# The low parts of the stream and of the wide factors, moved to other byte distances from the weights

## The reference

```python
for l in range(DEPTH):                        # first block, kernel layers 0 and 1
    h = rms_norm(x, mix_pre_norm[l])
    m = hybrid_mixer(h, w_in[l], ...)         # delta rule, pooling, retention, three gated branches, w_out
    x = x + rms_norm(m, mix_post_norm[l])
    h = rms_norm(x, ffn_pre_norm[l])
    x = x + rms_norm(swiglu(h, ffn_gate[l], ffn_up[l], ffn_down[l]), ffn_post_norm[l])
...
for l in range(DEPTH):                        # second block, kernel layers 2 and 3
    u = rmsnorm(h, attn_norm[l])
    h = h + hybrid_mixer_2(u, positions, w_in[l], ...)   # three attentions, three gated branches, w_o
    u = rmsnorm(h, mlp_norm[l])
    h = h + jnp.square(jax.nn.relu(u @ w_up[l])) @ w_down[l]
return rmsnorm(h, final_norm)
```

## Time and profile before

| | |
|---|---|
| time, median of 3 runs | 1875.27 us (1874.95 to 1875.65) |
| profiled execution: span from first to last instruction | 1875.1 us |
| TensorE matmuls, busy | 1841.3 us, 15,964 instructions |
| TensorE weight loads, busy | 1750.7 us |
| VectorE busy | 1259.6 us |
| ScalarE busy | 956.6 us |
| GpSimd busy | 307.3 us |
| read from HBM | 305.00 MB, 163 GB/s over the span |

### The profile page before, as it was taken

The page is one execution under the profiler, slowest core; times in us unless marked ns, Lnnn a source line. Parts: engine busy times, 40 slices in busy tenths (PEclk is TensorE's granted clock), DMA queues, the critical chain, the costliest instruction groups (busy, mean ns, idle before and its releaser), DMA issues.

```text
span 1875.1 us, 37406 instructions
## 1 busy us (share of the span) xinstructions
PE 1841.3 (98%) x15964; PEld 1750.7 (93%) x15964; DVE 1259.6 (67%) x1676; ACT 956.6 (51%) x1381; POOL 307.3 (16%) x176
## 2 busy tenths in 40 slices
PE   7999999999999999999999999999999999999998
PEld 7989998998888999999989999999999899999998
DVE  6884677665689557777648865676547785577643
ACT  5634466444563445554545455565434445555533
POOL 0050221000003212200002542310002352230000
PEclk9999999999999999999999999999999999999999
DMA  6443354656445334555656553456555663446652
GB/s 238 157 159 113 125 169 158 214 184 196 154 145 172 113 123 149 178 194 181 204 189 196 193 170 126 147 182 198 185 189 181 206 195 126 136 158 203 189 187 96
DMA packets 92165, 317.66 MB, mean 169 GB/s; under 512 B 11744, under 2 KB 12896, under 8 KB 91744
## 3 DMA queue, kind: packets, MB, share of 16 engines
q1 hardware_dynamic: 91424, 314.69, 51.7%
q10 hardware_dynamic: 576, 0.57, 0.1%
HBM read 305.00 MB, written 1.05 MB: 163 GB/s over the span
## 4 chain that ended last, share of the span: by engine, by line
PE 83%; DVE 12%; ACT 3%; issue 1%; DMA 1%; SPq 0%; DVEq 0%; ACTq 0%
PE bank L2007 82%; DVE wlo L1131 4%; DVE area L1131 3%; DVE area L1137 2%; ACT area L634 1%; ACT whi L640 1%; PE bank L2571 1%; DMA raw<-in_weights 1%; DVE hl L1137 1%; DVE xT L1137 1%; DVE area L1651 0%; DVE area L1649 0%; PE bank L2592 0%; ACT L622 0%; PE bank L2226 0%
## 5 line engine op out<-in xcount | busy, mean ns | idle before, releaser
L1131 DVE TENSOR_TENSOR wlo<-raw,whi 128x1024 fp32r<-128x1024 f32 x518 | 668.6, 1305 | 412.6 <-ACT whi L640 412.3
L2007 PE MATMUL bank<-hh,whi 128*128 128x256 f32 x2928 | 830.0, 284 | 18.5 <-DVE wlo L1131 15.9
L2007 PE MATMUL bank<-hh,wlo 128*128 128x256 f32 x2928 | 814.4, 279 | 0.0
L2007 PE MATMUL bank<-hl,whi 128*128 128x256 f32 x2928 | 807.2, 279 | 0.0
L640 ACT CAST whi<-raw 128x1024 fp32r<-128x1024 f32 x572 | 589.3, 1046 | 398.8 <-PE bank L2007 351.9
L2007 PEld LDWEIGHTS bank<-hh,whi 128*128 128x128 f32 x2928 | 551.3, 188 | 33.8 <-DVE wlo L1131 18.7
L2007 PEld LDWEIGHTS bank<-hl,whi 128*128 128x128 f32 x2928 | 551.1, 190 | 1.4 <-issue 1.4
L2007 PEld LDWEIGHTS bank<-hh,wlo 128*128 128x128 f32 x2928 | 551.4, 188 | 0.0
L1787 POOL TENSOR_TENSOR area<-area 128x512 f32<-128x512 f32 (+4 forms) x86 | 135.1, 1578 | 567.3 <-DVE area L1137 250.6
L1787 POOL TENSOR_TENSOR wlo<-raw,whi 128x1024 fp32r<-128x1024 f32 x54 | 133.9, 2481 | 384.7 <-ACT whi L640 384.7
L2007 PE MATMUL bank<-FH,whi 128*128 128x256 f32 x640 | 180.1, 281 | 0.0
(11 more groups left out here) (132 smaller groups left out, 1907.4 us busy)
## 6 DMA issues: line engine op xcount, KB each, us to landing
raw<-in_weights SPq DMA_DIRECT2D x572, 512.0 KB, 4.0
area<-area SPq DMA_DIRECT2D x96, 64.0 KB, 3.6
area<-area SPq DMA_DIRECT2D x16, 128.0 KB, 3.9
cst<-in_const SPq DMA_DIRECT2D x1, 1188.0 KB, 7.9
cst<-in_const SPq DMA_DIRECT2D x1, 1024.5 KB, 5.6
xT<-in_x SPq DMA_DIRECT2D x4, 256.0 KB, 7.9
out<-xT SPq DMA_DIRECT2D x4, 256.0 KB, 2.9
area<-in_lev SPq DMA_DIRECT2D x2, 384.0 KB, 6.8
```

Of the source, the lines that this page charges most:

```text
L1131: return v.tensor_tensor(dst, x, y, op)
L2007: return e.matmul(ps, x, y, start=start, stop=stop, skip_group_check=skip)
```

## The change

Each layer gets its own `hh`, `hl`, `FH` and `FL`, at addresses set modulo 512 relative to the first weight byte. For the high parts the distance is 192 in every layer, as before. For the low parts it is taken from a list by layer:

| layer | `hh`, `FH` | `hl` | `FL` |
|---|---|---|---|
| before, all | 192 | 192 | 192 |
| 0 | 192 | 224 | 64 |
| 1 | 192 | 160 | 0 |
| 2 | 192 | 0 | 224 |
| 3 | 192 | 64 | 160 |

The tensors of the four layers lie over one another, as one tensor did before. The stream's place is 512 bytes longer, which moves all behind it (`RSB`, `SW`, the work area) by 512 bytes. `FL` begins 32 to 480 bytes later in the area than its slot. Nothing else is changed; instructions, order and waits are the same.

```diff
+HIGH_PHASE = 192
+STREAM_PHASE = (224, 160, 0, 64)
+FACTOR_PHASE = (64, 0, 224, 160)
...
+        whi_at = at[0]
         whi = sb("whi", [P, RING, 1024], F32R)
...
-        hh = sb("hh", [P, 8, T], F32R)
-        hl = sb("hl", [P, 8, T], F32R)
+        stream = at[0]
+        at[0] += 2 * 4 * 8 * T + 512
...
-        def slot_r(name, i, k):
-            return sb(name, [P, k, T], F32R, offset=region + 4096 * i)
+        def slot_r(name, i, k, behind=0):
+            return sb(name, [P, k, T], F32R, offset=region + 4096 * i + behind)
+
+        def from_weights(first, by):
+            return (whi_at + by - first) % 512
+
+        hh, hl = ([sb(f"{name}{L}", [P, 8, T], F32R, offset=stream + by + from_weights(stream, STREAM_PHASE[L] if by else HIGH_PHASE))
+                   for L in range(2 * DEPTH)] for name, by in (("hh", 0), ("hl", 8192)))
...
-        FH, FL = slot_r("FH", 0, 32), slot_r("FL", 8, 32)
+        FH, FL = ([slot_r(f"{name}{L}", i, 32, from_weights(region, FACTOR_PHASE[L] if i else HIGH_PHASE)) for L in range(2 * DEPTH)]
+                  for name, i in (("FH", 0), ("FL", 8)))
```

Every use of the four names takes the tensor of its layer, for example:

```diff
-                    h = act(hh[:, k, :], xT[:, k, :], AF.Copy, scale=GAIN[norm][:, k:k + 1])
+                    h = act(hh[int(norm[-1])][:, k, :], xT[:, k, :], AF.Copy, scale=GAIN[norm][:, k:k + 1])
...
-                    return mm3(bank[m // 2][:, m % 2 * T:m % 2 * T + T], job.first + k, 128 * m, FH[:, k, :], FL[:, k, :],
+                    return mm3(bank[m // 2][:, m % 2 * T:m % 2 * T + T], job.first + k, 128 * m, FH[L][:, k, :], FL[L][:, k, :],
```

More of the change, by code:

```diff
@@ L851, in merge @@
                 a.wait_ge(*gated(name, L, 2 * j))
-                act(FH[:, 2 * j:2 * j + 2, :], v3(pair(YY, j)), AF.Copy, scale=0.5).then_inc(*a_br.up("sum", L, j))
+                act(FH[L][:, 2 * j:2 * j + 2, :], v3(pair(YY, j)), AF.Copy, scale=0.5).then_inc(*a_br.up("sum", L, j))
             def by_rows(name, L, settle={}):
@@ L932, in product @@
                     a.wait_ge(*v_ffn.at("product", L, i))
-                    a.copy(FH[:, i, :], FT[:, 512 * (i % 4):512 * (i % 4) + T]).then_inc(*a_ffn.up("high", L, i))
+                    a.copy(FH[L][:, i, :], FT[:, 512 * (i % 4):512 * (i % 4) + T]).then_inc(*a_ffn.up("high", L, i))
                 def ffn(m0):
@@ L1081, in mlp_high @@
                     a.wait_ge(*a_ffn.at("square", L, m0))
-                    a.copy(FH[:, m0:m0 + 2, :], v3(f)).then_inc(*a_ffn.up("high", L, m0))
+                    a.copy(FH[L][:, m0:m0 + 2, :], v3(f)).then_inc(*a_ffn.up("high", L, m0))
                 def mlp(m0):
@@ L1184, in low @@
                 for k in (2 * j, 2 * j + 1):
-                    x = stt(hl[:, k, :], xT[:, k, :], GAIN[norm][:, k:k + 1], hh[:, k, :].bitcast(F32), OP.mult, OP.subtract)
+                    x = stt(hl[int(norm[-1])][:, k, :], xT[:, k, :], GAIN[norm][:, k:k + 1], hh[int(norm[-1])][:, k, :].bitcast(F32), OP.mult, OP.subtract)
                 x.then_inc(*v_norm.up("low", norm, j))
@@ L1414, in merge @@
                 v.wait_ge(*a_br.at("sum", L, j))
-                stt(FL[:, 2 * j:2 * j + 2, :], v3(pair(YY, j)), 0.5, FH[:, 2 * j:2 * j + 2, :].bitcast(F32), OP.mult, OP.subtract).then_inc(*v_br.up("merged", L, j))
+                stt(FL[L][:, 2 * j:2 * j + 2, :], v3(pair(YY, j)), 0.5, FH[L][:, 2 * j:2 * j + 2, :].bitcast(F32), OP.mult, OP.subtract).then_inc(*v_br.up("merged", L, j))
             def by_rows(name, L, settle={}):
@@ L1531, in ffn_low @@
                     v.wait_ge(*a_ffn.at("high", L, i))
-                    tt(FL[:, i, :], f_(i)[:, 0:T], FH[:, i, :].bitcast(F32), OP.subtract).then_inc(*v_ffn.up("low", L, i))
+                    tt(FL[L][:, i, :], f_(i)[:, 0:T], FH[L][:, i, :].bitcast(F32), OP.subtract).then_inc(*v_ffn.up("low", L, i))
                 def product(i):
@@ L1751, in mlp_low @@
                     v.wait_ge(*a_ffn.at("high", L, m0))
-                    tt(FL[:, m0:m0 + 2, :], v3(f_(m0)), FH[:, m0:m0 + 2, :].bitcast(F32), OP.subtract).then_inc(*v_ffn.up("low", L, m0))
+                    tt(FL[L][:, m0:m0 + 2, :], v3(f_(m0)), FH[L][:, m0:m0 + 2, :].bitcast(F32), OP.subtract).then_inc(*v_ffn.up("low", L, m0))
                 def mlp(m0):
@@ L1820, in low @@
                 g.wait_ge(*g_norm.now())
-                tt(hl[:, 0:2, :], v3(pair(SQ2, 3)), hh[:, 0:2, :].bitcast(F32), OP.subtract).then_inc(*g_norm.up("low", norm))
+                tt(hl[int(norm[-1])][:, 0:2, :], v3(pair(SQ2, 3)), hh[int(norm[-1])][:, 0:2, :].bitcast(F32), OP.subtract).then_inc(*g_norm.up("low", norm))
             def delta(L):
@@ L2036, in parts @@
                         i = (at + m) % RING
-                        mm(bank[b][:, m * T:(m + 1) * T], whi[:, i, 128 * k:128 * k + 128], hh[:, k, :], (m, k) == (0, 0), False, True)
-                        mm(bank[b][:, m * T:(m + 1) * T], wlo[:, i, 128 * k:128 * k + 128], hh[:, k, :], False, False, True)
+                        mm(bank[b][:, m * T:(m + 1) * T], whi[:, i, 128 * k:128 * k + 128], hh[job.layer][:, k, :], (m, k) == (0, 0), False, True)
+                        mm(bank[b][:, m * T:(m + 1) * T], wlo[:, i, 128 * k:128 * k + 128], hh[job.layer][:, k, :], False, False, True)
                 for j in range(4):
@@ L2042, in parts @@
                         for k in (2 * j, 2 * j + 1):
-                            x = mm(bank[b][:, m * T:(m + 1) * T], whi[:, (at + m) % RING, 128 * k:128 * k + 128], hl[:, k, :], False, k == 7, True)
+                            x = mm(bank[b][:, m * T:(m + 1) * T], whi[:, (at + m) % RING, 128 * k:128 * k + 128], hl[job.layer][:, k, :], False, k == 7, True)
                         if j == 3:
@@ L2119, in by_token @@
                             ps = bank[job.banks[s]][:, :]
-                            xh, xl = hh[:, k, 128 * s:128 * s + 128], hl[:, k, 128 * s:128 * s + 128]
+                            xh, xl = hh[L][:, k, 128 * s:128 * s + 128], hl[L][:, k, 128 * s:128 * s + 128]
                             mm(ps, xh, wh, k == 0, False)
@@ L2139, in term @@
                     wh, wl = whi[:, i % RING, f:f + 512], wlo[:, i % RING, f:f + 512]
-                    xh, xl = FH[:, k, s:s + 128], FL[:, k, s:s + 128]
+                    xh, xl = FH[L][:, k, s:s + 128], FL[L][:, k, s:s + 128]
                     mm(bank[b][:, :], xh, wh, k == 0, False, True)
@@ L2472, in first @@
                 norm = f"mixpre{L}"
-                h = hh, hl, stream_ready(norm)
+                h = hh[L], hl[L], stream_ready(norm)
                 def sums():
@@ L2487, in first @@
                 for k in range(8):
-                    mm(bank[1][0:16, 0:T], SW[:, k, :], hh[:, k, :], k == 0, False, True)
-                    x = mm(bank[1][0:8, 0:T], SW[:, k, 0:8], hl[:, k, :], False, k == 7, True)
+                    mm(bank[1][0:16, 0:T], SW[:, k, :], hh[L][:, k, :], k == 0, False, True)
+                    x = mm(bank[1][0:8, 0:T], SW[:, k, 0:8], hl[L][:, k, :], False, k == 7, True)
                 x.then_inc(*e_dn.up("abrow", L))
@@ L2515, in first @@
                 norm = f"ffnpre{L}"
-                rest(project("gu", L, hh, hl, stream_ready(norm), lambda: norm_sum(norm), norm=norm))
+                rest(project("gu", L, hh[L], hl[L], stream_ready(norm), lambda: norm_sum(norm), norm=norm))
                 tokens("down", L, lambda k: v_ffn.at("low", L, k), f"ffnpost{L}", "mixpre1" if L == 0 else "attn2")
@@ L2601, in second @@
                 norm = f"mlp{L}"
-                rest(project("up", L, hh, hl, stream_ready(norm), lambda: norm_sum(norm)))
+                rest(project("up", L, hh[L], hl[L], stream_ready(norm), lambda: norm_sum(norm)))
                 by_rows("down", L, lambda k: v_ffn.at("low", L, k // 2 * 2), post("last") if L == 3 else None)
```

## The result

The changed kernel takes 1894.13 us (median of 4 runs, 1893.86 to 1897.03). The kernel before took 1875.46 us beside it. The ratio is 1.0108, with a 95% interval from 1.0085 to 1.013. I had forecast 1865 us and a gain. The time lies in the range, at the place of the first rival, and the direction is wrong.

A forecast was written before the change was run, and what follows sets the result against it. TensorE's start-to-start distance was taken to bound the kernel. Redrawn paces gain 12.0 us in slow stretches and lose 1.7 in fast ones, net -10: 1875.1 - 10.3 = 1865 us, range 1850 to 1902.

The forecast's parts named there:

- the first rival: Low part at its own distance brings stops into triples that have none: 1887 us for half, 1900 for all; chance 0.38.
- What bounds the kernel; two paces: Dense stretches: time is matmul count times start-to-start distance on TensorE, 113.4 or 117.8 ns with the same operands.
- Two stable interlocks: TensorE's stream: weight load and another matmul's moving operand interlock in two stable ways; low part's load 192 or 188 ns.
- How much is at the slower pace: Whole run, from mean weight-load durations: 1944 of 3568 triples slow; all fast would save 27 us with the wide ones.
- The draw: Long stretches draw their pace anew, two chances in three for 113.4 ns: gain 12.0 us, loss 1.7, net -10 us.
- The bound from above: TensorE: every triple that is now fast becomes slow, together +25 us; called not hard.
- The stretches' pace tied to one repeated start: Long stretches take 117.8 ns after one repeated start, two matmuls with ones for the norm, then the projection.
- The rival of new stops: Triples: a low part at its own distance breaks the evenness and adds stops; 1880 to 1923 us, chance 0.38.
- No effect: Distance doesn't matter on TensorE, the same interlocks come from the same starts: 1875 us, chance 0.17.
- Expected signs: By layer, equal distances in stream and factor should go the same way; a pace above 118 ns would refute the draw.

The follow-up runs named there:

- The triples alone: No layers, TensorE alone runs 52 families of triples over fixed data at various address distances; both parts at 192 gave 117.7 and 113.3 ns a matmul.
- the map: Triples alone at all 512 combinations of high-part, low-part and low-weight distances, two starts each; 4 of 1024 runs at 113.3 ns, the slowest 124.4.

## Why the prediction was wrong

- **What bounds the kernel; two paces** (right). TensorE's start-to-start distance is the time, and 113.4 and 117.8 ns were the two paces. No other engine's work grew by more than 2 us.
- **Two stable interlocks** (right that there are two paces). The triples alone show both from the same addresses. That the load of one matmul and the stream of another interlock is not shown, and the loads' duration, 192 against 188 ns, was no sign of it: in the slower kernel it was 189.
- **How much is at the slower pace** (too low). I had worked out 1944 of 3568 triples, 54%, from the mean duration of the loads. The starts in the trace of before, in unbroken rows of 24 or more matmuls, show 1873 of 2839, about two thirds.
- **The draw** (wrong, and this step carried the forecast). "If the shifted low part upsets the present interlock and every long stretch draws its pace anew, with two chances in three for 113.4 ns": the draw takes for granted that 113.4 ns is still among the lots. It exists at 4 of 1024 runs of the map, and at none of the four new pairs of high and low with the low weights in line. In the changed kernel every stretch with a moved low part went at 117.7 to 119.3 ns. The trace could have warned me only by its silence: it holds one distance, and I took over the odds of that one for all others. The gain of 12.0 us should have been 0, and the loss, 1190 x 4.4 ns x 1/3 = 1.7 us, should have been all triples that were at 113.4, and at 224 and 0 those at 117.8 as well.
- **The bound from above** (right in size). Every triple at 117.8 would be +25 us; measured +18.7. TensorE's busy time grew by 22.8 us, with 119.0 and 119.3 ns in layers 0 and 2 in it. Its idle time fell by 5.6 us, so a change of its pace does not come through whole, as I had said it would.
- **The stretches' pace tied to one repeated start** (wrong). The gate/up projections of layers 0 and 1 have the same two matmuls for the norm in them, and in the kernel before one went at 117.8 ns and the other at 113.4. Layer 3's stretch was at 117.8 ns in the kernel before and at 113.3 in another with the same distances. So the 1875 us of the kernel before were in part luck of the same kind; its runs lay between 1861 and 1879 us.
- **The rival of new stops** (right in outcome, 0.38). Its price, 1887 to 1900 us, holds the 1894. Its reason, that one part of three breaks the evenness, was wrong: with both parts at one new distance the time was 1892.1 us. What I held against it, the matmuls with 16 and 8 weight columns at 116.4 ns, was no evidence: what is loaded there is `SW`, which has an address of its own in steps of 64 bytes, so that row differs from a triple in shape, order and distance at once.
- **No effect** (wrong). The Trainium skill, in "TensorE: Matmul & The Clock Gate", Part 2, the step on LDWEIGHTS, says that loading the next weights doesn't take read bandwidth from the running matmul. The measurement decides against what I took from it, that no distance matters: with TensorE alone at work and only addresses changed, a matmul of 256 columns in this format goes at anything from 113.3 to 124.4 ns. Whether the two reads share anything is not shown by that.
- **Expected signs**: 224 in the stream and 224 in the factor did go the same way, 119.0 both, and so did 160 in the stream of layer 1 and in the factor of layer 3, 117.8 both. 0 and 64 can't be compared, as the factor has them in the first two layers, where it is the loaded operand. A pace above 118 ns was to mean that the draw between two paces is the wrong picture, and 119.0 and 119.3 came.

Shown: the cause is the distance among the addresses of the four operands (high and low weights, high and low activations), modulo 256. It is the relation of what is loaded to what is streamed, as moving the weights alone changed the pace in the way that moving both activations did. Not shown: which reads inside TensorE meet. A collision of the weight load and the stream in the same part of memory would fit the sharpness (4 bytes) and the 256-byte period, but no run separates it from another cause with that period. Open as well is what picks one of the two paces at 192.

## What to carry to other kernels

When TensorE goes back to back, work out the distance from start to start in each long stretch, and look for two values with the same operands: the longer one is an offer. Don't guess an address to get rid of it; a loop of the kernel's own matmuls over all distances takes one short run, and for the narrow form its numbers carried over to the kernel within a nanosecond. They don't say which of two paces a stretch will take, and the wide form's 233.3 ns at 192 was not among them. The median of a kernel with two such paces in it moved by a third of a percent between two comparisons (1875.46 and 1869.15 us for the same kernel here), so the paces in the trace are the surer measure.

## What the runs showed of the hardware that I had not expected

- In the high-low triples of 128 x 128 by 256 columns, the addresses alone move the pace from 113.3 to 124.4 ns, 10%, at a granted clock of 1.00, with a period of 256 bytes.
- With both activations at 192 and the low weights in line two paces are stable, 13.3 ns a triple apart. It isn't the only such place: in 58 of 512 address sets the two starts gave paces more than 1 ns apart.
- One more offset, 128 bytes between high and low weights, left only the shorter one in every long narrow stretch: 0.7% of the whole kernel for two lines.
- Moving the low part alone, the high part alone (which two of three matmuls stream) or both cost nearly the same: 1894.13, 1890.68 and 1892.1 us.
- TensorE waited less when its own stream was slower and more when it was faster: its idle time was 28.2 us in the slower kernel, 33.8 in the kernel before and 37.6 in the fastest.
